# Rows of the first gate in the arena instead of a ring place (hybrid attention and MoE step, one core)

## What is computed

```python
shift1, scale1, gate1, shift2, scale2, gate2 = modulation(c, p['w_mod'], p['b_mod'])
h = x * (1 + scale1) + shift1
... = project(h, p['w_in'])                      # three mixers in one projection
na_o, ret_o, diff_o = ...                        # neighbourhood attention, retention, differential attention
y = merge_mixers(na_o, ret_o, ret_g, diff_o, p, lam_init)              # ... @ p['w_out']
x = post_norm_residual(x, y, gate1, p['ln1_w'], p['ln1_b'])            # LN(ALPHA * x + gate1 * y)
h = x * (1 + scale2) + shift2
y = hier_moe(h, ...)                             # 32 SwiGLU experts, FF 256, two per token
x = post_norm_residual(x, y, gate2, p['ln2_w'], p['ln2_b'])
```

## Time and profile before

| | us |
|---|---|
| median of 3 runs | 1177.9 (1176.45 to 1179.03) |
| profiled execution, its own time | 1180.55 |
| its span, first to last instruction | 1178.6 |
| PE busy | 1086.1 (92%) |
| DVE busy | 429.7 (36%) |
| ACT busy | 211.5 (18%) |
| POOL busy | 178.8 (15%) |
| DMA, whole span | 342.77 MB, mean 291 GB/s |

### The profile page before, as it was taken

One profiled execution on the slowest core, in us unless ns is written; L12 is line 12 of the kernel. 1 busy time (PEld: TensorE's weight loads), 2 busy tenths in 40 slices (PEclk: granted clock), 3 DMA queues, 4 the chain that ended last, 5 costly groups with the idle time before them and its releaser, 6 DMA issues.

```text
span 1178.6 us, 16670 instructions
## 1 busy us (share of the span) xinstructions
PE 1086.1 (92%) x6670; PEld 714.3 (61%) x6671; DVE 429.7 (36%) x1029; ACT 211.5 (18%) x530; POOL 178.8 (15%) x180
## 2 busy tenths in 40 slices
PE   5899999989999999978989999999898999999784
PEld 1766878558756555545448567775687655555531
DVE  0034545266743111121162345442587312122116
ACT  0322324200111111110112233421002111111100
POOL 0442010041111111110113000201411111111001
PEclk8899999999989999998999999999998999999997
DMA  8999222497799999999999222237859999999981
GB/s 355 255 259 364 79 72 86 158 332 285 251 423 417 419 418 418 419 417 410 353 295 316 75 72 76 89 135 255 305 206 362 372 392 419 418 418 418 420 337 59
DMA packets 102624, 342.77 MB, mean 291 GB/s; under 512 B 20300, under 2 KB 61308, under 8 KB 70420
## 3 DMA queue, kind: packets, MB, share of 16 engines
q1 hardware_dynamic: 88400, 313.47, 69.9%
q0 software_dynamic: 12416, 18.79, 5.0%
q10 hardware_dynamic: 1732, 9.45, 2.0%
HBM read 337.76 MB, written 28.25 MB: 311 GB/s over the span
## 4 chain that ended last, share of the span: by engine, by line
PE 74%; DMA 9%; SPq 5%; issue 4%; DVE 3%; POOL 2%; ACT 2%; POOLq 0%; ACTq 0%; DVEq 0%
PE ps L1020 16%; PE ps L1317 16%; PE ps L1013 8%; PE ps L1197 8%; PE ps L1341 7%; SPq L875 5%; DMA arena<-in_exp_w_down 3%; PE ps L1281 3%; DMA ring<-in_exp_w_up 3%; DMA ring<-in_w_in 2%; PE ps L1274 1%; PE ps L1113 1%; PE ps L960 1%; PE ps L1381 1%; PE ps L1159 1%
## 5 line engine op out<-in xcount | busy, mean ns | idle before, releaser
L1317 PE MATMUL ps<-ring,arena 128*64 128x256 f32 x1376 | 199.2, 402 | 10.7 <-DMA ring<-in_exp_w_up 7.0
L1020 PE MATMUL ps<-ring,arena 128*128 128x256 f32 (+1 forms) x960 | 200.1, 367 | 6.2 <-DMA ring<-in_w_in 3.6
L1020 PEld LDWEIGHTS ps<-ring,arena 128*128 128x128 f32 x960 | 170.2, 194 | 29.0 <-issue 5.2
L1317 PEld LDWEIGHTS ps<-ring,arena 128*64 128x64 f32 x1376 | 119.8, 144 | 63.5 <-issue 21.9
L1013 PE MATMUL ps<-arena,ring 128*128 128x384 f32 x288 | 96.9, 490 | 0.7 <-ACT arena L1604 0.5
L2174 DVE TENSOR_TENSOR arena<-arena,ps 128x256 f32<-128x256 f32 x32 | 13.5, 422 | 226.5 <-PE ps L1317 150.9
L1197 PE MATMUL ps<-ring,arena 128*128 128x256 f32 x384 | 89.6, 397 | 0.0
L1341 PE MATMUL ps<-ring,arena 128*64 128x512 f32 x304 | 82.0, 611 | 4.7 <-DMA ring<-in_exp_w_down 3.2
L1197 PEld LDWEIGHTS ps<-ring,arena 128*128 128x128 f32 x384 | 76.7, 201 | 11.2
L1013 PEld LDWEIGHTS ps<-arena,ring 128*128 128x128 f32 x288 | 53.3, 190 | 36.8 <-issue 1.8
L2400 POOL DMA_INDIRECT arena<-token_rows,arena x30 | 30.6, 1019 | 272.1 <-PE ps L1281 141.7
(11 more groups left out here) (294 smaller groups left out, 1409.1 us busy)
## 6 DMA issues: line engine op xcount, KB each, us to landing
ring<-in_exp_w_up SPq DMA_DIRECT2D x48, 1024.0 KB, 22.7
ring<-in_w_mod SPq DMA_DIRECT2D x45, 1024.0 KB, 5.2
ring<-in_exp_w_gate SPq DMA_DIRECT2D x40, 1024.0 KB, 19.4
ring<-in_exp_w_down SPq DMA_DIRECT2D x39, 1024.0 KB, 26.1
ring<-in_w_in SPq DMA_DIRECT2D x24, 1024.0 KB, 14.3
arena<-in_exp_w_down SPq DMA_DIRECT2D x14, 1024.0 KB, 25.1
arena<-in_exp_w_gate SPq DMA_DIRECT2D x12, 1024.0 KB, 23.9
ring<-in_w_out SPq DMA_DIRECT2D x8, 1024.0 KB, 12.9
```

The lines of the kernel that those rows point to most:

```text
L1020: mm = pe.matmul(out[:, 0:w], hT[:, ch, where * P:(where + 1) * P], unit(l, name)[:, ch, 0:w], start=(ch == 0), stop=(ch == CH - 1))
L1317: mm = pe.matmul(ps[64 * w:64 * w + 64, 2 * (i % 2) + kind, 0:FF], xgT[i % 2][:, ch, w * SLOTS:(w + 1) * SLOTS], weights[:, ch * FF:(ch + ...
```

## The change

The rows of gate1 leave the ring: `row_tile` puts them at columns 0 to 2047 of the arena (GATE1 = 0), gate1 is no longer in ROW_FILLS nor among the releases, and `load_rows` waits for gate1 until PE's retention products (`ret_ready`) and DVE's last read and write of them (`ret_var`) are done for all three tiles. The order of SP's statements stays. Every later entry of the table of places moves.

```diff
--- before.py
+++ after.py
@@ -111,6 +111,7 @@
 
 C_NAO, C_RETO, C_DIFFO = C_DK, C_RK, C_DQ
 MIXT = 3072
+GATE1 = 0
 Z = 6144
 H2, H2T, XR, XGT = 10240, 7168, 7168, 9216
 PLACE_12, PLACE_13, PLACE_14 = 3072, 5120, 11264
@@ -202,7 +203,7 @@
 
 
 ROWS_LATE = {1: ("gate1", "shift2"), 2: ("scale2", "gate2")}
-ROW_FILLS = ("gate1", "shift2", "ln1", "scale2")
+ROW_FILLS = ("shift2", "ln1", "scale2")
 
 
 def front_order():
@@ -346,7 +347,7 @@
     gone += [u for u in fronts if LAST_JOB[u] < attended] + [("arena", BIAS_PLACE)]
     gone += [u for u in fronts if LAST_JOB[u] >= attended] + [("arena", SMALL_PLACE)]
     then = early_units(l + 1)
-    gone += [("wout", u) for u in range(OUT_UNITS)] + [("rows", "gate1")] + then[:4]
+    gone += [("wout", u) for u in range(OUT_UNITS)] + then[:4]
     gone += [("rows", n) for n in ("shift2", "scale2")] + [("arena", i) for i in (RING, RING + 1, CONST_PLACE)]
     gone += then[4:6] + [("arena", RING + 2)] + then[6:] + [("rows", "ln1")]
     return gone + EXPERT_RELEASES
@@ -527,6 +528,8 @@
         z = at(Z, D)
 
         def row_tile(l, name, k):
+            if name == "gate1":
+                return at(GATE1 + k * D, D)
             return places_of_unit[SPOT[l, ("rows", name)][0]][:, k * D:(k + 1) * D]
 
         def late_tile(l, name, k):
@@ -732,7 +735,7 @@
             elif kind == "wout":
                 eng.wait_ge(y_ready.sem, y_ready.at(l, TILES))
             elif kind == "rows":
-                done = {"gate1": gated, "ln1": ln1_done}.get(what[0], h2_ready)
+                done = ln1_done if what[0] == "ln1" else h2_ready
                 eng.wait_ge(done.sem, done.at(l, TILES))
             elif kind == "arena":
                 if what[0] == BIAS_PLACE:
@@ -780,8 +783,11 @@
 
             def load_rows(l, name):
 
-                before = SPOT[l, ("rows", name)][2]
-                wait_released(sp, *before)
+                if name == "gate1":
+                    sp.wait_ge(ret_ready.sem, ret_ready.at(l, TILES))
+                    wait_alone(sp, ret_var, ret_var.at(l, TILES))
+                else:
+                    wait_released(sp, *SPOT[l, ("rows", name)][2])
                 for k in range(2):
                     if name == "ln1":
                         src = (ln1_w, ln1_b)[k][l:l + 1]
```

## The result

| | us |
|---|---|
| after, median of 3 runs | 1191.12 (1188.61 to 1193.69) |
| before, the runs shown ahead | 1177.9 (1176.45 to 1179.03) |
| ratio after to before, 95% interval | 1.0107 (1.0092 to 1.0123) |
| after, profiled execution: own time, span | 1191.12, 1189.1 |
| after again beside before, six more runs | 1188.78 against 1178.83, ratio 1.0086 (1.0068 to 1.0104) |

Slower, as forecast, but by 13.2 us (10.0 in the repetition) and not by 6.4; 1191.12 lies above the range that ended at 1188.6. The two profiled executions differ by 10.5 us of span. In the changed kernel the lines have moved by 6: the projection is L1203, the transposes L1219, the logits L1225, the fold L2303 to L2305, h2 L2044, gate and up L1323.

A forecast was written before the change was run, and what follows sets the result against it. The prediction took TensorE's work (three quarters of the chain) and SP's fixed-order weight loads (DMA 9%) as bounds. Its terms 3.25 + 2.6 + 0.7 - 0.2 = 6.35, rounded +6.4, gave 1184.3 us, range 1178.8 to 1188.6.

The forecast's parts named there:

- (a) A place more: DMA's hole near 300 us: a free place moves 1 MB early, 0 to 2.5 us a layer; taken as -0.2 in all.
- DMA was dry at 322 us: Sign in the profile after: DMA still falls dry before its saturated stretch, where the lead of 1 MB is lost.
- (b) The wait: SP's queue: gate1 8.1 and 7.8 us late, less DVE's cover; PE idles 3.25 and 2.6 us before tile 0's transposes.
- The rival that the rows land sooner when issued later: SP's row loads: an emptier queue wins back the delay, so the time stays, 1177 to 1180 us; chance 0.13.
- some 14 us: Estimate by the skill's DMA cost for the six loads and scale2 with SP's issuing, 3.5 less than the rows.
- (c) The clock: PE at tile 0's transposes and logits: half-speed stretch moves (-0.5) or is added (+1.0 to 1.2); taken +0.35 a layer.
- (d) The end of layer 0: Layer 1's w_in units 0 and 1 leave SP later, waiting for pair 15: taken 0, bounds -1 and +1 us.
- more than the delay: Second half-speed stretch in both layers (+1.2 each) or gather suffers (+1), and last tile's steps slip: 1187 to 1191; chance 0.10.

The follow-up runs named there:

- after again: The changed kernel with no edit, run beside the kernel before on one chip: 1188.78 us, ratio 1.0086.
- Gate1 behind the second store: Changed kernel with gate1's waiting loads moved between the issue of the second store of modulation rows and the wait for its landing: 1175.82 us, ratio 0.9982.
- w_in as in the changed kernel: Kernel before; layer 1's w_in units 0 and 1 wait for pair 15's gate and down products: 1175.64 us, ratio 0.9980.
- With the transposes: 18 dummy PE transposes between tile 0's and tile 1's mixer transposes, added to each kernel of the pair: 1168.17 us (gate1 moved), 1170.02 us (w_in later).
- PE kept busy: Changed kernel with 28 dummy transposes on PE ahead of tile 0's transposes, in both layers: 1183.19 us, ratio 1.0030.
- Wait alone: Kernel before, gate1 still in its ring place and old table of places; only the waits for ret_ready and ret_var added: 1192.94 us, ratio 1.0121.
- late in layer 0 alone: Changed kernel, but in layer 1 gate1's loads stand behind the second store's issue; layer 0 keeps the changed order: 1181.89 us, ratio 1.0035.
- the kernel before with the transposes: Kernel before with 18 dummy PE transposes between the mixer transposes of tile 0 and tile 1: 1172.14 us, ratio 0.9945.

## Why the prediction was off

**(a) A place more, -0.2.** DMA was dry at 322 us (59 GB/s) as foreseen. "Gate1 behind the second store" has the place, "w_in as in the changed kernel" has not, and they take 1175.82 and 1175.64. With the transposes the pair differs by 2.1 us inside overlapping intervals. Right, or short by up to 2.

**(b) The wait, +3.25 and +2.6.** Right in every link, and in size in layer 0: 3.35 and, again, 3.42. In layer 1 PE idled 3.44 and 4.82. In the first trace, from gate1's issue to the fold it was 17.73 us, where I carried over 17.16 from the earlier trace rows, and SP was 8.0 late instead of 7.8: the 0.8 us missing. In the second the way to the fold was 19.3 us. The rival that the rows land sooner when issued later is refuted: 17.8 and 17.7 us, 17.6 and 19.3 in "after again". The Trainium skill's 2.0 us and 436 GB/s, from which I worked out some 14 us, stand there (DMA: Bandwidth & Descriptors, Anatomy of one DMA — SWDGE (gpsimd) path) for DMAs that GpSimd issues; these are SP's, and in no layer of either trace do the rows agree with that estimate.

**(c) The clock, +0.35 a layer. This is the step that failed.** I knew of one stretch at 1.2 GHz of 3.4 us and allowed that the idle time would move it or add one like it, +1.2 at most. It became one unbroken stretch of 10.2 us, in both layers of both traces. From the second tile's projection to the third one's end the changed kernel lost 6.5 and 6.4 us; less the idle times that is 3.15 and 2.96 of slower work. In layer 1 it is made up of the transposes (1.97 for 1.05, +0.9), the logits (3.63 for 1.97, +1.7) and the third tile (16.08 for 15.75, +0.3). The bound was wrong, not only the middle: I bounded a reaction of the clock by the reactions already in the trace, none of which followed an idle time this long at this place. "PE kept busy" shows it as cause and not companion.

The reading that I started from was unsound too: that the third tile is slow because PE idles ahead of it. In layer 0 of "w_in as in the changed kernel" the idle time ahead of it is the same, 0.73 us in front of the logits, and the tile ran at full speed:

```profile
293.97 14.06 PE L1200 MATMUL ps<-ring,arena 128*128 128x256 f32 x64
```

So did the third tile of layer 1 in "gate1 behind the second store" (14.06 us). In the kernel before the slow stretch on the third tile begins 34 us behind the start of the one on the first tile, in both layers (262.3 to 296.4, 839.1 to 873.3), and where the first was filled with transposes the third tile was fast as well. What sets off the second of the two is open.

**(d) The end of layer 0, 0.** I set off w_in's later issue as free, and looked only at PE's next need of w_in. That it also clears the way for the gather was named as a bound of -1 us; it was worth some 2.4.

**The sum.** Wait alone +14.1, the rest of the change -4.2: +10.0 in the repetition. My sum had +6.55 for (b) and (c), which in truth cost twice that, and -0.2 for the rest. Both errors were large, and the second hid part of the first. By the traces, (b) and (c) make 6.5 + 6.4 = 12.9, of which the waits are 6.8 for my 5.85 and the clock 6.1 for my 0.7; the stretch to layer 1 gives back 1.5. The rival "more than the delay" (1187 to 1191) named the right mechanism, at less than half its price, and had a chance of only 0.10.

## What to carry to other kernels

Ask of a wait on an issuing queue what stands behind it: the same wait cost 14 us ahead of the row loads, and nothing where the queue stood still anyway. A new idle time of PE is not priced by its length: here 3.4 us of it cost 6.5, and the bound of the clock's share must not come from shorter idle times. The mean clock of a whole run does not show this (0.961 after, 0.959 before); the windows behind the idle time do. And before a difference of 2 us in one stretch is explained, the same stretch of a repetition is worth a look. When loads change their releases, look at every transfer beside them, gathers too, not just at who needs the load next.

## What the runs showed of the hardware that I had not expected

A wait of 3.35 to 4.82 us on PE, with full-speed work up to it, was followed by 10.2 us at 1.2 GHz, in both layers and both traces of the changed kernel, although PE was busy for most of those 10.2 us (9.51 in the windows shown, 8.48 behind the wait of 4.82). Waits of 2.96 us ("late in layer 0 alone") and 3.22 us ("the wait alone", layer 1) had 10.2 us behind them too, one of 2.57 us 6.8 us. The Trainium skill (TensorE: Matmul & The Clock Gate, What's actually happening) says that the clock follows how busy PE has been and knows two states; the 0.50 in the one window and 1.00 in the stretches on either side agree with the two states. Why PE stayed at the lower one for 10.2 us of nearly unbroken work is open.

With the 2.1 us wait for POOL ahead of the second tile's mixer transposes, the first tile took 14.9 us and the third 15.6 in layer 0 of the kernel before, the second 14.0. With 2.1 us of transposes in place of the wait the first took 13.98 us and the third 14.06, though it begins 32 us behind the gap. How a gap reaches that far I have not separated. The slow stretches do not all vanish with the gap: in the kernel before with the transposes PE was granted 1.2 GHz from 313 to 320 us, where the kernel before ran at full speed, and the work between the third tile and the last tile's transposes took 11.8 us for 8.5.
